# Seven norms of a twelve-stage network: two units multiply the unnormalised input, 1/rms joins their eviction

## The chip, the cores and the metric

The kernel runs on one core of a Trainium2 chip. The metric is the device time of one execution in microseconds (us). The median of three runs of the kernel before is 3014.66 us (3008.84 to 3016.24).

## What is computed

A first network of four layers (pool, neighbourhood attention, conv, pool) works on 512 latent tokens `x` and 256 context tokens `ctx` with 1024 features; a second network of two layers (attention, Fourier mix and gated MLP side by side, then an MLP) works on the result and on another context. What matters here is what stands between the layers:

```python
def _rmsnorm(x, g):
    return x * lax.rsqrt(jnp.mean(x * x, axis=-1, keepdims=True) + EPS) * g

# first network, each of 4 layers
shift, scale, gate = _modulation(c, ada_w[i], ada_b[i])
hx = _rmsnorm(x, norm_g[i]) * (1.0 + scale[:, None]) + shift[:, None]
x = x + gate[:, None] * mixer(hx)          # mixer begins with hx @ w_in
...
return _rmsnorm(x, final_g)

# second network, each of 2 layers
px = modulate(rms_norm(x, g1), sh1, sc1) @ w_in
x = x + gt1 * mix_x
x = x + gt2 * squared_relu_mlp(modulate(rms_norm(x, g2), sh2, sc2), w1, w2)
```

So there are nine norms: one before each of the four mixers, the final one of the first network, and two in each layer of the second. Each is followed by products of the normalised, scaled and shifted `h` with weight matrices.

## The kernel before

Everything is kept transposed: features on the 128 partitions, tokens along the free axis. `x` is eight feature tiles of 512 tokens (`x_lat`) and eight of 256 (`x_ctx`); a stage works on T = TT = 768 tokens or T = TX = 512. Products are made in three passes of a high and a low part: `h_hi`, `h_lo` (names `Hh`, `Hl`) and `w_hi`, `w_lo` (`Wh`, `Wl`), 8 tiles of `h` against 8 tiles of a weight unit of 128x1024. One such product is a *unit*: 128 output features, 8 tiles x 3 passes.

`plan()` writes one list of steps. Each engine runs through that whole list in its order and does its part of every step, so that an engine never takes a later step before an earlier one. The steps that matter:

- `unit` (and `upart`, half of one): PE multiplies into one of two halves of the PSUM tensor `turns` (`PS`); a unit waits (`free_turn`) until the unit two turns back has been evicted. What evicts it depends on `ev`: ScalarE (ACT) for u, v, cg, sk, sq, sf; VectorE (DVE) or both for the rest. After a unit ACT rounds the weight of two units later (`round_unit(w + 2)`, L997) and DVE makes its low part (`split_unit`, L1199, output `w_lo`). There are two buffers for raw weights and two for `w_hi` and `w_lo`.
- `xupd`: the last units of a stage, whose eviction adds gate x product to `x` (DVE, L1202, output `x_lat`, `x_ctx`); ACT squares the new `x` (L1140), DVE adds the squares up in `tmp4` (L1199, output `tmp`).
- `ada` chunks ride on units: DVE multiplies 512 KB of modulation weights with the condition rows (L1213), once or, for sectors with a context row, twice.
- a norm, made by `norm()`: `gain` (DVE, small), `nstat` (PE sums over partitions, L837; ACT square root, L1048; DVE reciprocal and broadcast copy, L1342), `back` (PE transposes, L845, so that `scores` holds 1/rms for each token), then eight `ntile` steps: DVE multiplies x by gain and 1/rms (L1202, output `tmp`), ACT adds the shift and rounds (L1053, output `h_hi`), DVE makes `h_lo` (L1202). `norm()` puts `keep_warm` matmuls (L748) in front of `nstat`.
- the first two units behind a norm are *joined*: PE goes tile by tile through both, the second two tiles behind the first, as the `h` tiles arrive. Before a joined pair stand 8 `keep_warm` calls.
- `pool`: DVE makes windowed means of one u unit; ACT may evict the next u only when DVE is through with it.
- the first network's final norm (`final` steps) multiplies `x` itself, tile by tile, and sums the squares anew for the norm behind it.

In the attention of the first network, each head's bias (128 x 1792) is loaded once by the SyncE queue (SP), into one of two buffers. SP also goes through the list in order: weights (`w + 3` behind unit `w`), ada chunks, biases.

In the code of the mlp units, the eviction is this chain, which the steps of the prediction use:

```python
# ACT
chain(act.activation(T1[:, 0:t], ps[:, 0:t], ACT.Relu))
give(act.activation(Mh[:, m, 0:t], T1[:, 0:t], ACT.Square))
# DVE
chain(tt(T2[:, 0:t], T1[:, 0:t], T1[:, 0:t], ALU.mult))
done(rest(Ml[:, m, 0:t], T2[:, 0:t], Mh[:, m, 0:t]))
```

## Time and profile before

| | |
|---|---|
| median of three runs | 3014.66 us |
| the profiled execution | 3013.29 us, span 3011.5 us |
| PE matmul busy | 2808.6 us, 93% (with the keep-warm matmuls) |
| DVE busy | 1704.4 us, 57% |
| ACT busy | 936.8 us, 31% |
| DMA | 290 MB, mean 96 GB/s |

Times in a timeline are from the start of the span. A row is: start, duration, engine, line, operation, output <- inputs, shapes, how many, and in brackets how long the engine was idle before it and who ended the wait. PEclk is the granted TensorE clock, 1.00 for 2.4 GHz and 0.50 for 1.2 GHz. "turns" in a row is the PSUM tensor of the units, "scores" the other one.

### The profile page before, as it was taken

To read this page: it belongs to the slowest core of one execution; us is meant where nothing else is said; L and a number is where in the kernel's file an instruction comes from. 1 tells how busy PE (TensorE), PEld (TensorE's weight loads), DVE (VectorE), ACT (ScalarE), POOL (GpSimd) and SP (SyncE) were. 2 spreads that over 40 slices of the span, in tenths; PEclk is the share of its full clock that TensorE was granted. 3 is DMA by queue.
4 is the path that set the end of the run, shared out by engine and by line. 5 is a ranking of instruction groups with operands and counts; after the bars stand their busy time and mean duration, and the time that the engine had idled before them with its cause. 6 is when DMAs were issued, how large, how long until landed. Compare 5 with 4: busy or idle time off the path is not lost. (4 is left out here: it accounts for less than half of the span.)

```text
span 3011.5 us, 36579 instructions
## 1 busy us (share of the span) xinstructions
PE 2808.6 (93%) x14298; PEld 2325.1 (77%) x14298; DVE 1704.4 (57%) x2637; ACT 936.8 (31%) x1440; POOL 155.9 (5%) x84
## 2 busy tenths in 40 slices
PE   7998999999999987998988999999999899999999
PEld 6787777787877865776766778888888667878887
DVE  5786656666567878775545465443333546554343
ACT  2222344444232221332334332122122335332222
POOL 0000000000000000000035200000000006200000
PEclk8999999999999998998988999999999999999999
DMA  5242323333245543432300024322212120122333
GB/s 218 84 141 91 127 90 121 121 116 118 67 152 180 190 126 119 141 96 77 126 1 1 29 79 146 125 85 63 64 57 63 54 77 1 43 77 91 98 92 104
DMA packets 81626, 290.02 MB, mean 96 GB/s; under 512 B 9520, under 2 KB 12592, under 8 KB 80944
## 3 DMA queue, kind: packets, MB, share of 16 engines
q1 hardware_dynamic: 81456, 287.69, 29.1%
q8 instruction: 114, 1.87, 0.3%
q14 instruction: 56, 0.46, 0.0%
HBM read 285.56 MB, written 2.10 MB: 96 GB/s over the span
## 5 line engine op out<-in xcount | busy, mean ns | idle before, releaser
L756 PE MATMUL turns<-h_hi,w_hi 128*128 128x512 f32 (+1 forms) x2480 | 803.3, 373 | 70.8 <-DVE w_lo L1199 54.1
L756 PE MATMUL turns<-h_hi,w_lo 128*128 128x512 f32 (+1 forms) x2480 | 782.6, 365 | 0.0
L756 PE MATMUL turns<-h_lo,w_hi 128*128 128x512 f32 (+1 forms) x2480 | 780.0, 364 | 0.0
L756 PEld LDWEIGHTS turns<-h_hi,w_hi 128*128 128x128 f32 x2480 | 425.9, 193 | 178.1 <-DVE w_lo L1199 66.0
L756 PEld LDWEIGHTS turns<-h_hi,w_lo 128*128 128x128 f32 x2480 | 421.5, 192 | 75.0
L756 PEld LDWEIGHTS turns<-h_lo,w_hi 128*128 128x128 f32 x2480 | 422.0, 192 | 73.4 <-issue 1.1
L1199 DVE TENSOR_TENSOR w_lo<-w_raw,w_hi 128x1024 fp32r<-128x1024 f32 x300 | 366.8, 1223 | 141.3 <-ACT w_hi L997 141.0
L997 ACT ACTIVATE w_hi<-w_raw 128x1024 fp32r<-128x1024 f32 x300 | 315.4, 1052 | 384.5 <-PE turns L756 363.3
L711 POOL TENSOR_SCALAR tmp<-tmp,softmax_stats 128x768 f32<-128x768 f32 (+1 forms) x80 | 155.7, 1948 | 2432.6 <-DVE softmax_stats L1429 2432.3
L1202 DVE SCALAR_TENSOR_TENSOR x_lat<-turns,modulation,x_lat 128x512 f32<-128x512 f32 x112 | 84.1, 751 | 335.8 <-PE turns L756 335.8
L756 PE MATMUL turns<-m_hi,w_lo 128*128 128x512 f32 (+1 forms) x768 | 233.4, 358 | 0.0
L756 PE MATMUL turns<-m_hi,w_hi 128*128 128x512 f32 (+1 forms) x768 | 232.8, 357 | 0.0
L756 PE MATMUL turns<-m_lo,w_hi 128*128 128x512 f32 (+1 forms) x768 | 231.5, 356 | 0.0
L1213 DVE CUSTOM_DVE_ANT_0 ada_raw<-ada_raw,cond_rows,ada_bias 128x1024 f32<-128x1024 f32 x176 | 225.3, 1280 | 2.1 <-DMA ada_raw<-in_adapack 1.3
L1199 DVE TENSOR_TENSOR tmp<-tmp 128x768 f32<-128x768 f32 (+4 forms) x88 | 76.5, 870 | 253.9 <-ACT m_hi L1169 253.1
L748 PE MATMUL scores<-dft,ones 128*128 128x256 f32 x500 | 135.9, 421 | 15.7 <-DMA pool_edges<-in_edge 15.7
L756 PEld LDWEIGHTS turns<-m_hi,w_hi 128*128 128x128 f32 x768 | 126.7, 188 | 23.5
L756 PEld LDWEIGHTS turns<-m_lo,w_hi 128*128 128x128 f32 x768 | 126.4, 187 | 23.4
L756 PEld LDWEIGHTS turns<-m_hi,w_lo 128*128 128x128 f32 x768 | 127.4, 188 | 21.4
L1168 ACT ACTIVATE tmp<-turns 128x768 f32<-128x768 f32 (+1 forms) x64 | 45.2, 706 | 291.8 <-PE turns L756 290.0
L1140 ACT ACTIVATE tmp<-x_lat 128x512 f32<-128x512 f32 x56 | 35.4, 632 | 288.8 <-DVE x_ctx L1202 157.4
L748 PEld LDWEIGHTS scores<-dft,ones 128*128 128x128 f32 x500 | 101.6, 212 | 29.7 <-DMA pool_edges<-in_edge 15.7
(212 smaller groups left out, 3408.3 us busy)
## 6 DMA issues: line engine op xcount, KB each, us to landing
w_raw<-in_wpack SPq DMA_DIRECT2D x300, 512.0 KB, 3.5
ada_raw<-in_adapack SPq DMA_DIRECT2D x176, 512.0 KB, 4.4
bias<-in_bias SPq DMA_DIRECT2D x16, 896.0 KB, 4.5
ada_first_a<-in_adapack SPq DMA_DIRECT2D x12, 512.0 KB, 8.6
x_lat<-in_xT SPq DMA_DIRECT2D x1, 2048.0 KB, 9.0
x_ctx<-in_ctxT SPq DMA_DIRECT2D x2, 1024.0 KB, 8.9
ada_first_b<-in_adapack SPq DMA_DIRECT2D x4, 512.0 KB, 15.9
cond_rows<-in_crow SPq DMA_DIRECT2D x4, 512.0 KB, 10.5
```

Source lines behind the costliest of these rows:

```text
L711: pool.tensor_scalar(ex, ex, ST[:, x.qt % 2, 6:7], None, ALU.mult).then_inc(ex_scaled, 1)
L748: pe.matmul(dst, ONES[:], CS[:], start=True, stop=True)
L756: ins = pe.matmul(dst[:, lo:lo + sz], w, x[:, lo:lo + sz], start=first and n == 0, stop=last and n == 2)
L997: act.activation(Wh[:, w % 2, :], RAW[:, w % 2, :], ACT.Copy).then_inc(w_rounded, 1)
L1140: ins = act.activation(T1[:, lo:lo + sz], xseg(lo, m), ACT.Square)
L1168: chain(act.activation(T1[:, 0:t], ps[:, 0:t], ACT.Relu))
L1199: return dve.tensor_tensor(dst, x, y, op)
L1202: return dve.scalar_tensor_tensor(out=dst, in0=x, scalar=c, in1=y, op0=op0, op1=op1)
L1213: ins = dve.tensor_tensor_reduce(dump, ADR[:, n % 2, :], CROW[:, c, :], 0.5, ADAB[:, sect, k:k + 1], ALU.mult, ALU.add, MOD[:, sect, c, k: ...
```

## The change

All norms but the first are made anew, and some things around them:

- Instead of waiting for 1/rms, the first two units behind a norm multiply *raw* tiles: x times gain, rounded by ACT into `h_hi`, with `h_lo` made by DVE (step `raw`, eight of them). If the units before read `h` (src "H"), four or six raw tiles stand in front of the last `xupd` in the list and wait for `h_free`; otherwise one follows each `xupd`.
- The shift rides along as two more columns of `h` (for T = TX, the product is cut into pieces of 256 and 258 columns).
- The sums for 1/rms (`stat_sums`) and the transposes (`stat_back`) are put among the tiles of the raw pair. The eviction of the raw pair (`rawz`) multiplies by 1/rms into `ZT[0]`, `ZT[1]`; `rawb` adds the shift.
- The eight `ntile` steps then write the normalised tiles over the raw ones, each when the raw pair has read its tile, and the third and fourth units are joined instead.
- `w_hi` and `w_lo` get a third buffer: rounding and split go to `w + 3`, loads to `w + 4`. For the room, the attention's bias is loaded in 64 pieces of 128 x 640 into three buffers.
- The final norm of the first network is merged with the norm behind it: a second sum of squares is kept in the updates, and `final` steps multiply `x` later, beside the next units.
- In the attention stages k and v (sk and v) are the raw pair, q and g (sq and sf) the next one; other units shift accordingly. The keep-warm matmuls of these norms and pairs are gone.

```diff
+    def updates(src, T, sect, nxT, after=(), late=False, nxt=None):
+        def raw_tile(k):
+            s = add("raw", T=nxt[2], k=k, g=nxt[0], sect=nxt[1], src=src)
+            s.need = [gain, ups[k]] if k < len(ups) else [gain]
...
+        ahead = 4 if nxt is not None and nxt[2] == TT and T == TT else 6
+        for m in range(KT):
+            if nxt is not None and src == "H" and m == KT - 1:
+                gain = make_gain()
+                for k in range(ahead):
+                    raw_tile(k)
+            u = full(src, "xupd", T, m, after=after if m == 0 else (), sect=sect, nxT=nxT, late=late and m == 0)
...
+            if nxt is not None and src != "H":
+                if m == 0:
+                    gain = make_gain()
+                raw_tile(m)
...
+        for k in range(len(raws), KT - 1 if t == TX or final else KT - 2):
+            raw_tile(k)
+        nst = add("nstat", T=t, g=g, sect=sectn)
...
+        for k in range(len(raws), KT):
+            raw_tile(k)
+        back = add("back", T=t)
...
+        for k in range(KT):
+            tiles.append(add("ntile", T=t, k=k, g=g, sect=sectn))
+            if len(zs) < 2 and k >= (t == TT):
+                zs.append(add("rawz", T=t, half=len(zs)))
...
+        shifted = add("rawb", T=t)
+    def raw_pair(n, u, v):
+        raws, nst, back, tiles, zs, _ = n
+        for j, x in enumerate((u, v)):
+            x.after, x.raw, x.reader, zs[j].of = list(raws), j, zs[j], x
+        u.stats = (nst, back)
...
+        join(u, v)
-            hid = [full("H", "mlp", T, m, after=tiles if c == 0 and m < 2 else ()) for m in range(KT)]
+            hid = [full("H", "mlp", T, m, after=n[3] if c == 0 and m < 4 else ()) for m in range(KT)]
             if c == 0:
-                join(hid[0], hid[1])
+                raw_pair(n, hid[0], hid[1])
+                join(hid[2], hid[3])
-        Wh, Wl = sb("w_hi", [P, 2, D], F32R), sb("w_lo", [P, 2, D], F32R)
+        Wh, Wl = sb("w_hi", [P, 3, D], F32R), sb("w_lo", [P, 3, D], F32R)
...
 # PE
-                if v:
+                if s.warm:
                     keep_warm(8)
                 for x in (s, v) if v else (s,):
                     if x.part != 1:
                         pe.wait_ge(w_split, x.w + 1)
                         free_turn(x)
...
+                    if s.stats is not None and j == 3:
+                        stat_sums(s.stats[0])
+                    if s.stats is not None and j == (6 if s.stats[0].final else 5):
+                        stat_back(s.stats[1])
...
 # ACT
+                elif s.kind == "raw":
+                    act.wait_ge(dve_done, max(x.d1 for x in s.need))
+                    if s.src == "H" and s.k < KT - 1:
+                        act.wait_ge(h_free, (KT - 1) * freeing.index(s.of) + s.k + 1)
+                    for c, (lo, sz) in enumerate(segs(t)):
+                        ins = act.activation(Hh[:, s.k, lo:lo + sz], xseg(lo, s.k), ACT.Copy, scale=GA[:, c, s.k:s.k + 1])
+                    give(ins)
...
 # DVE
+                elif s.kind == "raw":
+                    take()
+                    for c, (lo, sz) in enumerate(segs(t)):
+                        ins = stt(Hl[:, s.k, lo:lo + sz], xseg(lo, s.k), GA[:, c, s.k:s.k + 1],
+                                  Hh[:, s.k, lo:lo + sz].bitcast(F32), ALU.mult, ALU.subtract)
+                    done(ins)
+                elif s.kind == "rawz":
+                    z = ZT[s.half]
+                    dve.tensor_copy(BC[:, s.half, :], ps[:, TT:TT + 2])
+                    if s.half == 0:
+                        chain(dve.tensor_copy(T3[:, 0:t], SP_[:, 0, 0:t]))
+                    if t == TT:
+                        done(tt(z[:, 0:TT], ps[:, 0:TT], T3[:, 0:TT], ALU.mult))
...
+                elif s.kind == "rawb":
+                    for j in range(2):
+                        for c, (lo, sz) in enumerate(segs(t)):
+                            ins = dve.tensor_scalar(ZT[j][:, lo:lo + sz], ZT[j][:, lo:lo + sz], BC[:, j, c:c + 1], None, ALU.add)
+                    done(ins)
...
+                if s.kind == "rawz":
+                    split_unit(s.of.w + 3)
+                if s.kind == "unit" and s.raw is None and turn_of_w[s.w] == s.turn:
+                    split_unit(s.w + 3)
```

## Rows read from the trace of the kernel before

**Rows 1.** The page's first part: busy time of each engine.
```profile
PE 2808.6 (93%) x14298; PEld 2325.1 (77%) x14298; DVE 1704.4 (57%) x2637; ACT 936.8 (31%) x1440; POOL 155.9 (5%) x84
```

**Rows 2.** The waits of PE: who, us in total, times, longest.
```profile
PE turns L756 <- DVE w_lo L1199: 55.0, 32, 7.4
```

**Rows 3.** Stretch 1098 to 1104: PE, PEld, DVE, ACT, POOL busy, then PEclk.
```profile
1098.00:1104.00 6.00, 6.00 (x20) 5.17 (x21) 2.09 (x5) 0.98 (x2) 0.00 (x0) 0.50 0.22 80
```

**Rows 4.** Timeline of the norm before the first MLP, T = 768.
```profile
1768.41 3.62 PE L748 MATMUL scores<-dft,ones 128*128 128x256 f32 x16
1768.71 0.75 DVE L1202 SCALAR_TENSOR_TENSOR x_lat<-turns,modulation,x_lat 128x512 f32<-128x512 f32 x1 [2.71 <-PE turns L756]
...
1770.94 1.03 DVE L1199 TENSOR_TENSOR tmp<-tmp,tmp 128x512 f32<-128x512 f32 x2 [1.08 <-ACT tmp L1140]
1771.89 1.23 DVE L1199 TENSOR_TENSOR w_lo<-w_raw,w_hi 128x1024 fp32r<-128x1024 f32 x1
...
1775.56 0.56 DVE L1342 COPY tmp<-rms 128x768 f32<-128x768 f32 x1
1776.18 1.16 PE L845 MATMUL scores<-ident,tmp 128*128 128x128 f32 x6 [0.39 <-DVE tmp L1342]
...
1777.48 0.75 DVE L1202 SCALAR_TENSOR_TENSOR tmp<-x_lat,gain_cols,scores 128x512 f32<-128x512 f32 x1 [1.36 <-PE scores L845]
...
1779.89 1.15 DVE L1202 SCALAR_TENSOR_TENSOR h_lo<-tmp,modulation,h_hi 128x512 fp32r<-128x512 f32 x2 [0.22 <-ACT h_hi L1053]
...
1796.36 1.15 DVE L1202 SCALAR_TENSOR_TENSOR h_lo<-tmp,modulation,h_hi 128x512 fp32r<-128x512 f32 x2 [1.29 <-ACT h_hi L1053]
```

**Rows 5.** Timeline behind it: evictions of the MLP units; L1168 begins each.
```profile
1799.00 0.81 ACT L1168 ACTIVATE tmp<-turns 128x768 f32<-128x768 f32 x1 [2.77 <-PE turns L756]
...
1802.81 0.81 ACT L1168 ACTIVATE tmp<-turns 128x768 f32<-128x768 f32 x1 [1.17 <-DVE m_lo L1199]
...
1812.84 0.81 ACT L1168 ACTIVATE tmp<-turns 128x768 f32<-128x768 f32 x1 [7.39 <-PE turns L756]
...
1821.32 0.81 ACT L1168 ACTIVATE tmp<-turns 128x768 f32<-128x768 f32 x1 [5.84 <-PE turns L756]
```

**Rows 6.** Timeline, the same stretch of the second MLP, T = 512.
```profile
2638.53 0.75 DVE L1202 SCALAR_TENSOR_TENSOR x_lat<-turns,modulation,x_lat 128x512 f32<-128x512 f32 x1 [1.73 <-PE turns L756]
...
2657.93 0.75 DVE L1202 SCALAR_TENSOR_TENSOR h_lo<-tmp,modulation,h_hi 128x512 fp32r<-128x512 f32 x1 [0.89 <-ACT h_hi L1053]
```

**Rows 7.** Timeline of ACT behind it: the second and the fourth unit's evictions.
```profile
2662.67 0.60 ACT L1168 ACTIVATE tmp<-turns 128x512 f32<-128x512 f32 x1 [0.64 <-DVE m_lo L1199]
...
2676.75 0.60 ACT L1168 ACTIVATE tmp<-turns 128x512 f32<-128x512 f32 x1 [3.23 <-PE turns L756]
```

**Rows 8.** Timeline: conv's seventh and last update on DVE, pool layer's third u on ACT.
```profile
1086.89 0.75 DVE L1202 SCALAR_TENSOR_TENSOR x_lat<-turns,modulation,x_lat 128x512 f32<-128x512 f32 x1
...
1092.91 0.75 DVE L1202 SCALAR_TENSOR_TENSOR x_lat<-turns,modulation,x_lat 128x512 f32<-128x512 f32 x1
...
1136.04 0.60 ACT L1124 ACTIVATE u_padded<-turns 128x512 f32<-128x512 f32 x1 [6.80 <-DVE d_lo L1199]
```

**Rows 9.** Timeline: the pool layer's last update, and the final norm's last sum.
```profile
1308.76 0.75 DVE L1202 SCALAR_TENSOR_TENSOR x_lat<-turns,modulation,x_lat 128x512 f32<-128x512 f32 x1
...
1326.02 0.69 DVE L1199 TENSOR_TENSOR tmp<-tmp,tmp 128x512 f32<-128x512 f32 x1 [0.80 <-ACT tmp L1058]
```

**Rows 10.** Timeline, second network: ends of the eighth unit, each layer (second sf).
```profile
1447.44 0.81 ACT L1160 ACTIVATE fourier_in<-turns 128x768 f32<-128x768 f32 x1 [6.56 <-PE turns L756]
...
2424.12 0.60 ACT L1160 ACTIVATE fourier_in<-turns 128x512 f32<-128x512 f32 x1 [3.89 <-PE turns L756]
```

**Rows 11.** Timeline: DVE at attention's last update before, PE's first transposes behind it.
```profile
326.75 0.75 DVE L1202 SCALAR_TENSOR_TENSOR x_lat<-turns,modulation,x_lat 128x512 f32<-128x512 f32 x1 [2.87 <-PE turns L756]
...
381.61 1.08 PE L899 MATMUL scores<-ident,tmp 128*128 128x128 f32 x4 [2.42 <-DVE v_lo L1199]
```

**Rows 12.** Timeline: one ada chunk on DVE, before the first MLP.
```profile
1764.72 1.28 DVE L1213 CUSTOM_DVE_ANT_0 ada_raw<-ada_raw,cond_rows,ada_bias 128x1024 f32<-128x1024 f32 x1
```

More of the change, by code:

```diff
@@ L77, in __init__ @@
         self.swap = False
+        self.raw, self.stats, self.warm, self.frees, self.need, self.final, self.tiles, self.own = None, None, False, False, [], False, None, False
 ACT_ONLY, DVE_ONLY = {"u", "v", "cg", "sk", "sq", "sf"}, {"cv", "cb"}
@@ L86, in ends_in @@
     if s.kind in ("upart", "scores", "trans", "pvmm", "back", "cond_rows"):
+        return None
+    if s.kind == "unit" and s.ev == "v" and s.raw is not None and s.layer is not None:
         return None
@@ L461, in plan @@
             s.turn = turn
-        elif s.of is not None:
+        elif s.of is not None and s.kind not in ("raw", "rawz", "ntile"):
+            s.turn = s.of.turn
+    for s in steps:
+        if s.kind == "rawz":
             s.turn = s.of.turn
@@ L1017, in _ @@
                 prev = s
[L1018 removed]
+                if s is None or s.kind in ("cond_rows", "upart", "adared", "pool", "spgate", "adape", "scores", "trans", "pvmm", "back", "gnorm", "gain", "adafirst", "rawz", "rawb", "final"):
+                    continue
+                if s.kind == "unit" and s.ev == "v" and s.raw is not None and s.layer is not None:
                     continue
```

386 lines of the change are left out of this document (232 added, 154 removed).

## The prediction

> **What bounds the kernel now.** I read the page first: PE's matmuls are busy for 93% of the span and DVE for 57% [rows 1], so nearly everything costs what it costs PE, except where PE waits. Then PE's waits: the largest in sum is on the low part of a weight, 55 us in 32 waits [rows 2]. Then timelines around the eight norms in question. The one before the first MLP [rows 4] shows the pattern. The last update's matmuls end at 1768.4 (the keep-warm matmuls begin). DVE finishes x and the sum of its squares at 1771.97, PE's transposes of 1/rms begin at 1776.18, and the first tile of h is complete at 1781.0. The last is at 1797.5, so one tile takes (1797.5 - 1781.0)/7 = 2.35 us: an ACT operation and a DVE operation (1.15 us) that wait for each other. The pair that reads them needs 2 x 8 tiles of PE; a whole unit takes 1821.32 - 1812.84 = 8.48 us [rows 5], 1.05 us a tile, so 16.8 us. From 1768.4 to the pair's end, about 1802 (its second eviction begins at 1802.8 [rows 5]), that is 33.6 us for 16.8 us of products. At 512 tokens everything is about two thirds. So the norms do hold idle PE time (some 120 us in sum), but inside them DVE and ACT set the pace, not PE. That decides the rest.
>
> **Norm before the first MLP, step by step (T = 768).** DVE is free 2.71 us before the update starts at 1768.71, so at 1766.0 [rows 4]. New in front of that update: gain and shift columns (six operations on 8 to 16 columns; the nearest row is the copy of 768 columns at 0.56, so below 3.4 and above 0; as they are tiny I take 0.8), ACT's first raw tile (1.1 us, from 0.81 for 768 columns in one operation [rows 5] and two operations here), four raw tiles on DVE at 1.15. They end at 1772.6, so the update, and with it the sum, comes 3.9 us later: at 1775.9. The raw pair can't begin sooner: PE waits for the turn of its second unit, which is that last update. The stretch from 1768.4 to 1775.9 has no keep-warm matmuls any more.
> PE then: four raw tiles 4.2, sums 1.5, four tiles 4.2, transposes 1.1 [rows 4], plus a clock charge of 2.5 (below): 1/rms stands in PSUM at 1789.4. It stood there at 1777.3. The sums' way through ACT and DVE (1776.12 - 1771.97 = 4.15, less 1.35 for split and gain = 2.8) lies beside the second four tiles. From PSUM to the first normalised tile 3.7, as before (1777.3 to 1781.0): 1793.1. Second tile 1795.5. Then `rawz` 1.7 (copy of 1/rms, 0.6 by the copy row of 0.56, and a multiply of 0.96), and because a weight split (1.23) now follows it, the next tile comes 1.2 + 1.15 + 1.15 = 3.5 later; the second `rawz` costs 1.0 and 3.5 again: 1805.2. Four more tiles 9.4: 1814.6. `rawb` (four operations) 1.7: 1816.3. The PE side of the second pair, 16.8 us from 1802, ends at about 1819 to 1820 and is not late.
> What is late next are the evictions, because every engine takes the list in order: the raw pair's outputs may be processed only behind `rawb`. First unit 3.8 (1802.81 - 1799.00 [rows 5]), two ada chunks 2.5 [rows 12], DVE half of the second 1.9, third unit 3.6: 1828.1. PE's fifth unit waits for that turn. It started at 1821.2 (fourth unit's end). Lost: 6.9, and a clock charge of 2.5 since PE sat idle again for 8 us. Term: +9.4.
>
> **The other norms, by the same steps.** Second MLP (T = 512, six raw tiles in front of the update): DVE free at 2638.53 - 1.73 = 2636.8 [rows 6]; 0.8 + 0.6 + 6 x 0.75 gives 2642.7, update 4.2 later, sum at 2644.9; PE 2.8 + 2.5 + 1.0 + 2.8 + 0.7 gives 2654.7; the raw unit's end 3.5 later, 2658.2, now leads: `rawz` 1.2 and 2.7, second 0.8 and 2.7: 2665.6; five tiles at 1.55: 2673.4 (before 2658.7 [rows 6]); `rawb` 1.1; three evictions of 2.8 (2662.67 begins the second [rows 7]): 2682.9 against 2676.5 [rows 7]. Term +6.4 + 2.5 = +8.9.
> Conv: its norm has no raw tiles in front of the update; the eight raw tiles ride in the updates and fit (0.8 lag); then raw pair, tiles, cv's four operations and two chunks before cb frees its turn: 3.5 later, + 2.5 clock. Term +6.0.
> Second pool layer: here DVE is already the bound in the updates before: they start 1092.91 - 1086.89 = 6.02 us apart [rows 8] where PE needs 5.6. Seven raw tiles add 0.75 each, gain, memset and shift 1.7: the sum is 7.0 later. Then 29.5 to the end of `rawb`; u's eviction, chunks and window means follow on DVE. Saved: two rounds and splits (4.6) and 1.2 behind the last u. The third u's eviction, at 1136.04 [rows 8], comes 10 later. Term +8.8.
> Final norm and the one behind: the second square and sum add 1.3 to seven updates (9.2), six raw tiles and gain 9.0: the update of 1308.76 [rows 9] comes at 1327.0, its sum at 1330.5. The final norm's own stretch is gone, which ended at 1326.7 [rows 9]. So this start is 3.8 later, and 46 us behind it four units are done instead of two. Up to the eighth unit (1447.3 before [rows 10]) three unit-and-head steps of 15.5 and one head remain, with `final` (1.5 a step) on DVE in their way: 1449.6. Term +2.3.
> Second network's second layer: no raw tiles in front, evictions on ACT alone; the raw pair covers v, and sk's head, which ran uncovered, lies beside a half unit. Eighth unit at 2419 against 2424 [rows 10]. Term -5.0.
> Neighbourhood attention: free at 326.75 - 2.87 = 323.9 [rows 11], update 3.9 later, `rawb` 40.3 behind the sum: 374.2. Then k, v, q, g are evicted in one go, with five chunks and splits between, and the first softmax has no unit beside it: transposes at 389.9 against 381.6 [rows 11]. Term +8.3.
> Third weight buffer: the long wait of 7.4 [rows 2] shrinks by 2.3 only, since the turn's eviction is late there too; two pool layers save 1.2 each; no other of the 55 us goes, as most lie in the u stretches, where ACT's eviction, round, DVE's split and window means are a closed loop whatever the number of buffers. With small ones, -5. The 64 bias loads have two steps of lead: 0, and up to 1 us on each of 28 ada chunks if a 512 KB load comes late behind them; that stays in the range.
> Sum: 9.4 + 8.9 + 6.0 + 8.8 + 2.3 - 5.0 + 8.3 - 5 = +33.7. Against the profiled execution's own 3013.3 (1.4 below the median) that is 3047.
>
> **The clock charge.** Behind PE's wait that ended at 1097.5 the granted clock is 0.50, 1.2 of 2.4 GHz [rows 3]; the row covers 6 us, in which 3 us of products are lost. The kernel before has keep-warm matmuls against that, which go. I take 2.5 for each restart behind a wait like that one or longer, in seven raw pairs and three restarts behind evictions, 25 us in all; bounds 0 and 3.4 each, 34 in sum.
> The Trainium skill ("TensorE: Matmul & The Clock Gate", What's actually happening) says that for modelling the ramp penalty is under 1% of a typical span. By it alone the charge would be dropped and the sum would be +9, 3022; the row of 0.50 speaks against that for a kernel that adds seven such waits.
>
> **Rivals.** (a) Faster: the raw pair fills PE's idle time and ACT and DVE keep up. That needs the evictions of the raw pair to end before PE's fourth unit; then each norm keeps what its idle time gives, 33.6 less 16.8 less 7.5 that remain in front, some 9 us at 768 and 5 at 512 tokens, and the final norm's 16: near 65, so 2950 to 2990. For it: half of each norm is idle PE. Against it: the tile pace of 2.35 us starts 12 us later and has 5.7 us of `rawz` and splits in it. "Perfetto Trace Analysis" (Optimization Strategies) of the Trainium skill has this rule, to keep the matmul engine utilised and to relieve the engine that blocks; the first half speaks for the change, the second against it, since DVE gets more work. (b) No difference: restarts cost nothing, or the list hides the evictions better than I count: +9 to -9, 3004 to 3022. (c) Worse than forecast, and slower than before: the SP queue, which now waits for each softmax step, hands ada chunks out late; from about 3 us of delay DVE waits in each of 28 units: +30 on top, 3077.
>
> **Chances and numbers.** Forecast (slower, 3030 to 3066) 0.68; (a) 0.16; (b) 0.12; (c) 0.04. A measurement of this kernel tells 0.3%, 9 us, from no change. Faster 0.16, same 0.12, slower 0.72. Range 2992 to 3066: it leaves out (c) and most of (a); the forecast's own is 3030 to 3066.
>
> **What would show it.** In the profile after: first tile of h (L1202) some 12 us later behind each sum; the update in front of the raw pair starting 4 us behind PE's end; PE waiting for evictions (an `m_lo`, a `conv` operation) before the fifth unit; DVE's busy time up by some 90 us; 0.50 clocks behind each norm. If PE's fifth unit starts without a wait, (a) is true. If updates of the conv layer stay 6.0 us apart, the pool term is wrong.

## The result, and the profile after

The changed kernel takes 3080.27 us (median of four, 3077.68 to 3092.32), before 3015.45 beside it: ratio 1.0217 [1.0193, 1.0241]. Timed once more later, it was 1.0207 [1.0184, 1.0229]. So it is 62 to 65 us slower, where 34 were forecast; the direction was right, the size was not, and 3080 lies above the forecast's range (2992 to 3066). The profiled execution took 3082.5 us, its span is 3080.7.

The changed kernel's page, answering to [rows 1], and then the mean granted clock of before and of the changed kernel:

```profile
PE 2775.9 (90%) x14134; PEld 2307.7 (75%) x14134; DVE 1786.1 (58%) x2814; ACT 984.5 (32%) x1526; POOL 155.9 (5%) x84
```
```profile
core 0: 3011.5 us, clock 0.960
```
```profile
core 0: 3080.7 us, clock 0.945
```

PE is busy 33 us less (the keep-warm matmuls are gone), DVE 82 us more (forecast about 90). PE's waits by line and releaser (us in total, times, longest), answering to [rows 2]:

```profile
PE turns L817 <- DVE tmp L1317: 66.4, 16, 17.7
PE turns L817 <- ACT u_padded L1239: 36.1, 10, 12.6
PE turns L817 <- DVE raw_out L1317: 28.5, 7, 6.5
PE scores L940 <- DVE tmp L1527: 26.8, 14, 4.9
```

The 55.0 us for the low part of a weight are gone. In their place stand waits that the forecast named: for the sum of squares in front of the raw pair (seven of the 16 waits for `tmp` L1317, 56.4 us of the 66.4), and for the raw pair's first output (`raw_out`), seven times, once a norm.

PE's busy time from the first product of `h` to the end; the columns are the stretch, its length, PE busy (matmuls), clock, DMA share and GB/s. Before, then the changed kernel:

```profile
69.96:3011.50 2941.54, 2758.26 (x14024) 0.96 0.29 93
```
```profile
78.92:3080.70 3001.78, 2714.99 (x13860) 0.95 0.29 93
```

So PE is idle 287 us there in place of 183: the change adds 104 us of waits and takes away 43 us of busy time, keep-warm matmuls above all.

The norm before the first MLP in the changed kernel, answering to [rows 4] and [rows 5]; a bracket at a PE row is its wait:

```profile
1826.39 0.75 DVE L1320 SCALAR_TENSOR_TENSOR x_lat<-turns,modulation,x_lat 128x512 f32<-128x512 f32 x1
...
1829.90 0.98 PE L817 MATMUL turns<-h_hi,w_hi 128*128 128x512 f32 x2 [7.67 <-DVE tmp L1317]
...
1843.27 0.75 DVE L1320 SCALAR_TENSOR_TENSOR tmp<-x_lat,gain_cols,scores 128x512 f32<-128x512 f32 x1 [1.15 <-PE scores L841]
...
1845.74 1.15 DVE L1320 SCALAR_TENSOR_TENSOR h_lo<-tmp,modulation,h_hi 128x512 fp32r<-128x512 f32 x2 [0.28 <-ACT h_hi L1171]
...
1867.26 1.15 DVE L1320 SCALAR_TENSOR_TENSOR h_lo<-tmp,modulation,h_hi 128x512 fp32r<-128x512 f32 x2 [1.29 <-ACT h_hi L1171]
1868.51 1.42 DVE L1469 TENSOR_SCALAR raw_out<-raw_out,raw_shift 128x512 f32<-128x512 f32 x4
...
1882.36 0.98 PE L817 MATMUL turns<-h_hi,w_hi 128*128 128x512 f32 x2 [7.74 <-DVE m_lo L1317]
```

The update stands behind four raw tiles, 4.1 us after PE's last product of it (1822.2). The sum stands at 1829.65 (the row of x is followed by its square and the sum, 3.3 us). From there the first normalised tile is complete 17.2 us later and the last 38.7 us, to the tenth what the forecast has (1775.9 to 1793.1 and 1814.6); that some ten steps add up to the tenth is luck, that they stand in this order is not. PE waits 7.67 us (forecast 7.5) for the raw pair, reads the last normalised tile by 1874.6, and then waits 7.74 us for the eviction that frees the fifth unit's turn (forecast 8 to 9: from 1819 or 1820 to 1828.1).

Here the steps of the forecast can be read off one by one. The other terms come from marks: the first update of `x` on DVE in each stage. The table gives them in us. The shift is taken from the first product of `h`, which is 9.0 us later in the changed kernel's profile (78.92 against 69.96; see the section on the hardware). "Of this step" is the shift less that of the row above, so a row holds the norm in front of its stage and the rest of the stretch between the two marks.

| first update of | before | after | shift | of this step | forecast |
|---|---|---|---|---|---|
| first pool layer | 267.4 | 276.1 | -0.3 | -0.3 | third buffer |
| neighbourhood attention | 804.0 | 823.2 | 10.2 | 10.5 | 8.3 |
| conv | 1050.7 | 1077.7 | 18.0 | 7.8 | 6.0 |
| second pool layer | 1266.5 | 1307.0 | 31.5 | 13.5 | 8.8 |
| second network, first attention | 1710.5 | 1763.2 | 43.7 | 12.2 | 2.3 |
| first MLP, first block | 1863.7 | 1926.8 | 54.2 | 10.5 | 9.4 |
| first MLP, fourth block | 2269.4 | 2329.5 | 51.1 | -3.1 | third buffer |
| second attention | 2600.5 | 2655.5 | 46.1 | -5.0 | -5.0 |
| second MLP, first block | 2704.1 | 2769.5 | 56.4 | 10.3 | 8.9 |
| second MLP, fourth block | 2969.1 | 3038.1 | 60.1 | 3.7 | third buffer |

The seven norms cost 59.8 us against 38.7 forecast; the rest, which the forecast put at -5 for the third buffer, is +0.3. In a second profile of the changed kernel each step is within 0.2 us of these, but for the first, 3.2 us larger. So a mark is good to about 3 us, and so is a sum of them. The marks give 60 us and the times 62 to 65; where the rest lies is open, since the profiles tell nothing of the other executions.

### The profile page after: what moved, and what is told of

The parts are those of the page before. It is cut to its first block and busy times, and to the rows that moved or that the text cites. A ratio compares the mean times of both kernels' runs of the same rounds, so it can differ in the third digit from the quotient of the medians.

```text
span 3080.7 us, 36741 instructions
## 1 busy us (share of the span) xinstructions
PE 2775.9 (90%) x14134; PEld 2307.7 (75%) x14134; DVE 1786.1 (58%) x2814; ACT 984.5 (32%) x1526; POOL 155.9 (5%) x84
## 5 line engine op out<-in xcount | busy, mean ns | idle before, releaser
L817 PE MATMUL turns<-h_hi,w_hi 128*128 128x512 f32 (+1 forms) x2528 | 817.3, 375 | 163.2 <-DVE tmp L1317 60.2
L817 PE MATMUL turns<-h_lo,w_hi 128*128 128x512 f32 (+1 forms) x2528 | 801.0, 369 | 0.0
L817 PE MATMUL turns<-h_hi,w_lo 128*128 128x512 f32 (+1 forms) x2528 | 797.6, 367 | 0.0
L817 PEld LDWEIGHTS turns<-h_hi,w_hi 128*128 128x128 f32 x2528 | 442.1, 198 | 261.8 <-issue 180.6
L817 PEld LDWEIGHTS turns<-h_lo,w_hi 128*128 128x128 f32 x2528 | 440.2, 197 | 78.1 <-issue 1.5
L817 PEld LDWEIGHTS turns<-h_hi,w_lo 128*128 128x128 f32 x2528 | 439.3, 196 | 78.5
L1317 DVE TENSOR_TENSOR w_lo<-w_raw,w_hi 128x1024 fp32r<-128x1024 f32 x300 | 366.7, 1223 | 108.2 <-ACT w_hi L1092 108.1
L1317 DVE TENSOR_TENSOR tmp<-tmp 128x768 f32<-128x768 f32 (+4 forms) x88 | 76.5, 870 | 245.2 <-ACT m_hi L1287 244.3
L1331 DVE CUSTOM_DVE_ANT_0 ada_acc<-ada_raw,cond_rows,ada_bias 128x1024 f32<-128x1024 f32 x88 | 112.6, 1280 | 2.2 <-DMA ada_raw<-in_adapack 1.3
L1317 DVE TENSOR_TENSOR pt_lo<-turns,pt_hi 128x768 fp32r<-128x768 f32 (+1 forms) x80 | 67.9, 849 | 61.1 <-ACT pt_hi L1201 59.9
## 6 DMA issues: line engine op xcount, KB each, us to landing
cond_rows<-in_crow SPq DMA_DIRECT2D x4, 512.0 KB, 10.3
```

The lines of the kernel that those rows point to most:

```text
L817: ins = pe.matmul(dst[:, at:at + sz], w, x[:, lo:lo + sz], start=first and n == 0, stop=last and n == 2)
L1317: return dve.tensor_tensor(dst, x, y, op)
L1331: ins = dve.tensor_tensor_reduce(dump, ADR[:, n % 2, :], CROW[:, c, :], 0.5, ADAB[:, sect, k:k + 1], ALU.mult, ALU.add, MOD[:, sect, c, k: ...
```

## Experiments

All ratios are to the kernel before, timed beside each. "By the marks" is the shift of the last mark from before, as in the table (60.1 for the changed kernel, 63.2 in its second profile); it comes from one execution, the ratio from four or more. Where the two differ, both are given.

### The parts that are not norms

All eight norms as before on the changed kernel, so that the third weight buffer, the loads four units ahead and the bias pieces are left:

```diff
+        if nxt is not None and nxt[0] in OLD:      # OLD = (1, 2, 3, 4, 5, 6, 7)
+            for m in range(KT):
+                full(src, "xupd", T, m, ...)
+            return old_norm(nxt[2], nxt[0], nxt[1])
```

> All eight norms as before; only the third buffer of w_hi and w_lo, the loads four units ahead and the 64 bias pieces of the change are kept. Theory A (the prediction's term): 5 us faster than before, 3010, with the 7.4 us wait for w_lo in the conv layer gone. Theory B (from the two traces: the attention steps keep their pitch, the MLP blocks at 768 tokens gain 1.0 each, those at 512 lose 1.2 each, the conv stage loses 2): between 0 and 3 us slower, 3015 to 3018. The start of the program, whose instructions are the same in all kernels, took 9 us longer in the changed kernel's profile: if the buffers or the bias do that, it is here too, and the time is 3024.

Measured 0.9994 [0.9976, 1.0013], by the marks -2.5 us: no difference that the times show, and neither theory is excluded by them alone. The 7.4 us wait of the conv layer is still 4.9, as the forecast had it (2.3 less). But PE's idle time from the first product of `h` on is 180 us (183 before): where PE waited for `w_lo` in the pool layers, it now waits about as long for ACT's eviction of the u before (`u_padded`). So the savings that the forecast had there didn't come. (In this kernel and the next the weights of the attention stages lie in another order than the units, so these layers multiply by each other's columns; their operations are those of the right order.)

With this run as the base in place of before, the seven norms cost 11.2, 9.1, 12.3, 11.9, 10.3, -3.3 and 11.0 us in the order of the table, 62.5 in sum.

The same with `OLD = (1, 2, 3, 4, 6, 7)`, one norm new:

> As the run with the buffers alone, but the norm ahead of the second network's second layer is made the changed kernel's way (raw pair sk and v, then sq and sf). The traces of before and after give a term of -5.1 us for that stretch and +5.6 us for the stage behind it, of which 4.2 were forecast. Theory A (the terms are local): 5 us faster than the run with the buffers alone. Theory B (the gain is given back in the half units and attention steps behind it): within 2 us of it.

1.0015 [0.9996, 1.0034], by the marks -5.2, that is 2.7 us less than the run above: by the times no difference can be told. The marks put it in the norm's own stretch (-5.2 there against -1.7), and the stretches behind it gain or lose nothing more. Even the one norm that gained is no gain that a measurement shows.

### The place of the tiles

```diff
-        Hh, Hl = sb("h_hi", [P, KT, TT + 2], F32R), sb("h_lo", [P, KT, TT + 2], F32R)
+        Hh, Hl = sb("h_hi", [P, KT, TT], F32R), sb("h_lo", [P, KT, TT], F32R)
```

> The run with the buffers alone (all eight norms as before, third weight buffer, 64 bias pieces), but with h tiles 768 words apart, as before, in place of 770: the two shift columns that only the changed norms need are gone. In the trace of the run with 770, a product of 512 columns of h starts 225 to 240 ns after the one ahead of it, in a pattern that repeats every eight tiles; in the trace of before it is 227 ns always. Theory A (the place of the tiles in memory sets the pace of the products): 2480 products of 512 columns get 4.5 ns faster and some 700 tiles of 768 tokens 4 ns, 14 us in all: 3002 where before has 3016. Theory B (the third weight buffer makes the pattern): as the run with 770 words, 2 us faster than before.

0.9959 [0.9942, 0.9975], by the marks -17.5: theory A, and this kernel is faster than before and than the changed kernel. Two stretches of eight units in the second MLP (192 products of 512 columns each, nothing else on PE), first of `h`, then of `m`, with the columns as above. Before, then the run with 770 words, then 768:

```profile
2743.02:2786.55 43.53, 43.53 (x193) 1.00 0.28 86
2786.55:2831.34 44.79, 44.79 (x193) 1.00 0.33 105
```
```profile
2742.57:2787.15 44.58, 44.58 (x194) 1.00 0.29 85
2787.15:2832.12 44.97, 44.97 (x193) 1.00 0.34 104
```
```profile
2730.98:2774.51 43.53, 43.53 (x193) 1.00 0.30 86
2774.51:2819.49 44.98, 44.98 (x193) 1.00 0.34 105
```

At the same clock and with PE never idle, eight units of `h` take 43.53 us with tiles 768 words apart and 44.58 with 770: 227 and 232 ns a product. That is the price of the room for the shift columns at 512 tokens, and the forecast had nothing for it. At 768 tokens, where pieces of 512 and 256 columns take turns, it isn't paid everywhere: a block of the first MLP takes 134.4 us with 768 words and 134.2 with 770.

What makes the 12 us against before is not the waits either. From the first product of `h` on, with 770 and with 768 words:

```profile
75.52:3014.70 2939.18, 2758.71 (x14024) 0.97 0.30 95
```
```profile
75.84:3000.00 2924.16, 2738.45 (x14024) 0.97 0.30 96
```

PE is idle 180 and 186 us (183 before), and busy 2759 and 2738 (2758 before). So the gain lies in the pace of the products, part of it in less half clock, and not in fewer waits for a buffer. Such a run also moves all other tensors: the block of the first MLP, in which PE is never idle, went from 135.3 us to 134.4 with them. How much of the 12 us is owed to the third buffer and how much to the places, no run took apart.

With 800 words in the changed kernel:

> The changed kernel with h tiles 800 words apart in place of 770, nothing else. Theory A (the place of the tiles in memory sets the pace): 11 to 14 us faster than the changed kernel. Theory B (pace set by the three weight buffers): no change. Either way the waits of the norms stay as they are.

1.0196 [1.0163, 1.0229], by the marks 63.1: nothing, and eight units of `h` keep their mean of 232 ns a product. This excludes neither the place of the tiles nor the buffers as the cause: 800 words, like 770, put the eight tiles at eight different places modulo 1024 bytes, 768 words at one. With 768 words and the shift columns left out:

> The changed kernel with h tiles 768 words apart and without the two shift columns in the products: the raw pairs' outputs lack the shift (a column of the product stands in for it, so that every other operation is the same). With 800 words in place of 770 nothing had changed. Theory A (only with 768 words, the same place modulo 1024 bytes for each tile, do products of h start every 227 ns; the kernel with norms as before gained 15 us by it): 12 to 15 us faster than the changed kernel. Theory B (in the changed kernel the waits of the norms hide it, since its products of h stand partly in them): 5 us or less.

1.0155 [1.0135, 1.0175], by the marks 53.0: 16 to 19 us less than the changed kernel by the times, 7 by the marks. Eight units of `h` in the second MLP, in the changed kernel and here:

```profile
2808.54:2853.11 44.57, 44.57 (x193) 1.00 0.28 85
```
```profile
2801.82:2845.38 43.56, 43.56 (x193) 1.00 0.27 86
```

The pace comes back in the changed kernel too, with its three buffers, so the place of the tiles makes it. Whether it is worth 7 or 17 us these runs don't settle.

In the fast kernel (768 words, norms as before), all later tensors moved by 864 bytes:

> The kernel with the norms as before, third weight buffer and h tiles 768 words apart (0.9959 of before), with all tensors of the later stages moved by 864 bytes, so that the m tiles lie at the same place modulo 1024 bytes as the h tiles, whose products at 512 columns start every 227 ns; those of m start every 234 ns now. Theory A (place modulo 1024 bytes sets the pace): the products of m at 512 columns go to 227 ns, 5 us, and the time to 0.994 of before. Theory B (h and m differ for another reason, say what wrote them): pace and time stay.

0.9948 [0.9928, 0.9968], by the marks -14.7: as fast as without it. But the pace did as said; `m`, then `h`:

```profile
2696.67:2740.19 43.52, 43.52 (x193) 1.00 0.34 107
2740.19:2783.71 43.52, 43.52 (x193) 1.00 0.28 87
```

The products of `m` at 512 tokens went from 44.98 us to 43.52 by their place alone. At 768 tokens the same move made them slower (a block of the first MLP takes 135.7 us, 1.3 more), and both about cancel.

### The clock

> The changed kernel with keep-warm matmuls put in front of the raw pair, the second pair and the fifth unit of each norm, about as many as fill 80% of PE's wait there. Theory A (the clock charge of 2.5 us a restart, 25 in the sum): 15 to 25 us faster than the changed kernel, 3055 to 3065. Theory B (ACT and DVE set the pace of these stretches, so that PE's half clock behind a wait is mostly hidden in waits that follow): 5 us or less, 3075 to 3080.

1.0291 [1.0267, 1.0314], by the marks 87.7: 22 to 25 us slower than the changed kernel by the times, so neither theory is tested. One keep-warm call is two matmuls; they outlasted the waits and held PE up (around the first MLP's norm PE isn't idle at all). With 40% as many, and then once more beside the changed kernel:

```diff
+                if s.keep:
+                    keep_warm(s.keep)              # 12, 6, 12 at the first MLP norm
```

> As the run with keep-warm matmuls, which was 23 us slower than the changed kernel since each call is two matmuls and the calls outlasted the waits; here 40% as many (12, 6 and 12 at the first MLP norm), so that they end inside the waits. Theory A (the clock charge, 2.5 us a restart): 15 to 25 us faster than the changed kernel. Theory B (ACT and DVE set the pace of these stretches): 5 us or less.

> The changed kernel itself once more, beside the three kernels of this call, so that they are compared on one chip. Its profile tells how far two executions of the same instructions differ: the start (until the first product with h) took 70.0 to 79.3 us in the profiles so far, and the time that PE's products lose at half clock behind it 98 us in before and 115 in the changed kernel. If those are chance, both move here; if the change makes them, they stay at 79 and 115.

> The changed kernel with keep-warm matmuls that end inside the waits, as before, timed beside the changed kernel. Its profile had 16.5 us less of products at half clock than the changed kernel's, and the same span behind the first product; its times were 0.44% lower, with an interval as wide. Theory A (the clock charge is real, about 16 us of it): 10 to 16 us faster than the changed kernel. Theory B (ACT and DVE set the pace, so that nothing is gained): within 4 us of it.

Changed kernel again: 1.0207 [1.0184, 1.0229], by the marks 63.2. With keep-warm: 1.0173 [1.0142, 1.0204] and 1.0175 [1.0155, 1.0195], so 10 to 13 us less each time, though the intervals still overlap. By the marks it is 60.5 and 55.8, 0 to 7 us less: 4.4 less in the conv step and 2.8 in the first MLP's, both times, but 4.2 more in the second attention's. The first MLP's norm in the second of these, with PE's waits in front of the raw pair, the second pair and the fifth unit:

```profile
1823.57 0.59 PE L827 MATMUL turns<-h_hi,w_hi 128*128 128x512 f32 x2 [2.49 <-DVE tmp L1329]
1847.12 0.59 PE L827 MATMUL turns<-h_hi,w_hi 128*128 128x512 f32 x2 [1.74 <-DVE raw_out L1329]
1873.50 0.98 PE L827 MATMUL turns<-h_hi,w_hi 128*128 128x512 f32 x2 [4.07 <-DVE m_lo L1329]
```

Two of three restarts now go at full clock (0.59 us for two products, not 0.98), and from the raw pair to the fifth unit it is 49.9 us, where it was 52.5. What is lost to half clock can be added up in two ways, from the first product of `h` on. PE's busy time, times the share of the clock that wasn't granted, is 98 us in before, 121 and 123 in the two profiles of the changed kernel, 102 in both with keep-warm. What the pace of gapless products loses against the usual one of their kind is 98, 115 and 116, and 99, a sum that hangs on what is taken as usual. So the change loses 17 to 25 us of products to half clock, and at most some 10 to 13 of them are time. The charge is real; 25 was about twice too much.

The Trainium skill ("TensorE: Matmul & The Clock Gate", What's actually happening) puts the ramp penalty under 1% of a typical span. For what the change adds this holds: 10 to 13 us are 0.3 to 0.4% of 3080. For all of it it doesn't: 98 us are 3.3% of the span of before. By the page alone the sum was 3022, further from what came than with the charge.

The changed kernel's second profile also has a first product of `h` at 79.0 us, as the first had. By the expectation that would make the late start the change's own. But kernels with the changed norms have theirs at 69.2 to 70.1 us in three other profiles, and one with the norms as before at 79.1: the start isn't the change's. The half clock is.

### DVE's list in front of the sum

```diff
-        ahead = 4 if nxt is not None and nxt[2] == TT and T == TT else 6
+        ahead = 2
```

> The changed kernel with two raw tiles in front of the last update in place of four (768 tokens) or six (512). In the trace of after, DVE is free 2.5 us ahead of the update in front of the first MLP and four raw tiles then hold the update up 4.1 us. Theory A (the raw tiles in front of the update are the delay): 2.5 to 3 us less in each of the four norms concerned, 3068 to 3071. Theory B (raw tiles behind the update then hold up the raw pair as much): no change, 3080.

1.0158 [1.0135, 1.0181], by the marks 48.1: 15 to 18 us less by the times, 12 by the marks: 0.1, 6.9, 3.1 and 3.7 in the steps of the four norms with such tiles, and 2.2 more in the first pool layer, which the edit doesn't touch. (In the neighbourhood attention the wait in front of the raw pair is 2.5 us shorter, but the step isn't.) PE's wait in front of the first MLP's raw pair is now

```profile
1812.84 0.98 PE L817 MATMUL turns<-h_hi,w_hi 128*128 128x512 f32 x2 [5.18 <-DVE tmp L1317]
```

against 7.67. So theory A: the raw tiles put in front of the last update were a delay, and those behind it weren't late.

### DVE's list behind the raw pair

```diff
+        elif skip[0]:                              # skip[0] = 4 behind each norm
+            skip[0] -= 1
+            owed[0] += 1
+            chunks = 0
```

> The changed kernel, but the first four units behind each of the seven norms take no modulation chunk; later units take two until the debt is paid. In the trace of after, DVE has two chunks (2.7 us) between the shift step and the eviction for which the fifth unit of the MLP waits, and ten chunk operations (12.8 us) ahead of the first head's 1/rms in the second network's first layer. Theory A (DVE's list behind the raw pair is the path): 15 to 25 us faster than the changed kernel. Theory B (the debt costs as much later, or ACT is the path): within 5 us.

Both theories fall: 1.0248 [1.0227, 1.0269], 12 us slower than the changed kernel. The fifth unit of the first MLP still waits 7.03 us (7.74), so the chunks there were hardly on the path. The loss is mostly in the second network's heads. By the marks (74.0) the first attention takes 10.6 us more than in the changed kernel; the neighbourhood attention takes 4.9 more and the conv step 3.7 less, and why is open. PE's head sums there, for sk and sq0 to sq3, in the changed kernel and in this one:

```profile
1420.23 1.39 PE L948 MATMUL scores<-head_ones,sk_square 128*128 128x2 f32 x12
1439.97 1.39 PE L948 MATMUL scores<-head_ones,tmp 128*128 128x2 f32 x12
1454.41 1.40 PE L948 MATMUL scores<-head_ones,tmp 128*128 128x2 f32 x12
1471.96 1.39 PE L948 MATMUL scores<-head_ones,tmp 128*128 128x2 f32 x12
1490.75 1.40 PE L948 MATMUL scores<-head_ones,tmp 128*128 128x2 f32 x12
```
```profile
1423.82 1.39 PE L953 MATMUL scores<-head_ones,sk_square 128*128 128x2 f32 x12
1436.74 1.39 PE L953 MATMUL scores<-head_ones,tmp 128*128 128x2 f32 x12
1457.24 1.40 PE L953 MATMUL scores<-head_ones,tmp 128*128 128x2 f32 x12
1477.68 1.39 PE L953 MATMUL scores<-head_ones,tmp 128*128 128x2 f32 x12
1498.12 1.39 PE L953 MATMUL scores<-head_ones,tmp 128*128 128x2 f32 x12
```

The first step is shorter (12.9 us from 19.7, no chunks ahead of it), but the three behind it went from 14.4, 17.6 and 18.8 to 20.4 or 20.5: two chunks, both twice, now stand ahead of each head's 1/rms on DVE. In sum that is 3.8 us more; the other 7 lie in front of these rows and behind them, and were not taken apart. The debt was moved, in part, to where DVE is the path.

### The final norm

The final norm and the one behind it as before, `OLD = (4,)`:

> The changed kernel with the first network's final norm and the norm behind it made as before, one after the other, and the second network's first layer in its old order of units. From the start of the pool updates to the first update behind the attention, the changed kernel is 12 us slower than the one with all norms as before; the forecast had 2.3. Theory A (raw tiles in front of the last pool update, six heads' steps with modulation chunks and final steps in front of them on DVE): 10 to 13 us faster than the changed kernel. Theory B (the stretch behind catches up): under 5 us.

1.0179 [1.0148, 1.0209], 9 to 11 us less than the changed kernel: theory A by the times. By the marks it is 14 less at the first attention's update and at the end of the first MLP, but only 3.6 at the end: in the second attention of this execution 8 us more than in before's are lost at half clock, in the changed kernel's 1.5 us less. That looks like chance of the execution and not like the edit, since the kernel with three edits below, which has this one too, has -3.6 us in that step; no second profile was taken.

In the next kernel the final norm is merged again, and its eight `final` steps stand further back:

```diff
-            if both and len(finals) < KT:
-                finals += [add("final", k=len(finals) + j, T=TX) for j in range(2)]
+            if both and e == "su":
+                finals += [add("final", k=len(finals) + j, T=TX) for j in range(4)]
```

> The changed kernel, but the eight final steps of the merged norm (each pair 1.6 us on DVE) stand behind the units su0 and su1, where no head follows, and not in front of four heads' 1/rms. The step from one unit to the next was 17.6 to 18.8 us there against 15.5 forecast. Theory A (the final steps are in the heads' way): 5 to 7 us faster than the changed kernel. Theory B (the half units wait for ACT and PE's half clock, not for DVE): under 2 us.

1.0211 [1.0189, 1.0232]: nothing by the times. By the marks it is 71.7, 8 to 12 us slower than the changed kernel, 6.5 of them in the first attention's step. And yet theory B is wrong, which had the final steps in nobody's way. The same head sums, sk to sq3, and the transposes behind them:

```profile
1418.71 1.39 PE L948 MATMUL scores<-head_ones,sk_square 128*128 128x2 f32 x12
1438.30 1.40 PE L948 MATMUL scores<-head_ones,tmp 128*128 128x2 f32 x12
1451.20 1.39 PE L948 MATMUL scores<-head_ones,tmp 128*128 128x2 f32 x12
1466.82 1.39 PE L948 MATMUL scores<-head_ones,tmp 128*128 128x2 f32 x12
1480.73 1.40 PE L948 MATMUL scores<-head_ones,tmp 128*128 128x2 f32 x12
...
1514.14 1.54 PE L957 MATMUL scores<-ident,raw_out 128*128 128x128 f32 x6 [10.76 <-DVE x_lat L1320]
```

From the second one on, the sums are 12.9, 15.6 and 13.9 us apart (the last two 14.8 and 13.8 in before), and from the first to the last it is 8.5 us less than in the changed kernel. So the final steps were in their way. But the final steps now hold the part of `scores` that the next transposes need, and PE waits 10.76 us for that: a gain turned into new waits that are at least as long.

### Sums of edits

The norms of the conv layer and of the second pool layer as before, `OLD = (2, 3)`:

> The changed kernel with the norms in front of the conv layer and of the second pool layer made as before, the other five in the new way. In the traces the two terms are 9 and 12 us (forecast 6.0 and 8.8), the conv updates being 7.2 us apart in place of 6.0. Theory A (the terms are local): 18 to 22 us faster than the changed kernel, 1.0140 of before. Theory B (part of them is lost again behind them): 12 us or less.

1.0134 [1.0114, 1.0153], by the marks 39.2: 22 to 25 us less by the times, 21 to 24 by the marks, with 9.5 less in the conv step and 12.7 in the second pool layer's. Theory A: these terms are local.

Two tiles ahead, keep-warm and the final norm apart, together:

> The three edits that helped alone, together: two raw tiles in front of the last update (-15 us by the ratios), keep-warm matmuls that end inside the waits (-10), the final norm apart (-9). Theory A (they work in different places and add up): 1.0207 - 0.0050 - 0.0032 - 0.0030 = 1.0095 of before, 3048. Theory B (ACT and DVE behind the raw pair are the bound, and what one mend gives the next one loses): 1.013 or more.

1.0126 [1.0109, 1.0144], by the marks 34.9: 24 to 27 us less by the times, where the three alone sum to between 33 and 42. That lies between the two theories: part of it adds up, part doesn't, and the interval leaves open how much. Even so this kernel is 38 us slower than before, and 50 behind the kernel with 768 words, which has no raw pair.

## Why the prediction was right, and where it was wrong

**What bounds the norm.** Right: not PE but the tile pace of DVE and ACT, and the evictions behind it. PE idles 7.67, 4.33 and 7.74 us in the first MLP's norm, in front of the raw pair, the second pair and the fifth unit, where the kernel before kept it warm or busy. So rival (a), which had PE's fifth unit start without a wait, is excluded, and (b) by the times.

**First and second MLP, attention.** 9.4, 8.9 and 8.3 forecast, 10.5, 10.3 and 10.5 measured. The mechanism stands (the update 4.1 us behind PE, forecast about 4; the fifth unit's wait in the MLPs). In the MLPs the run with two tiles ahead changes what the steps said it would. Only the sizes are 1 to 2 us short. One of the signs was put wrongly: the first tile of `h` is 12 us later on the clock in the forecast, but behind the sum it is 17.2 us in place of 9.0, so 8 later.

**Second attention.** -5.0, as forecast, but in part by luck: 1.8 of it is there with the buffers alone, and by the run with this norm alone the rest isn't worth a difference that the times show.

**Conv and second pool layer.** 6.0 and 8.8 forecast, 7.8 and 13.5 measured; the run without both confirms the sum. The conv updates were taken as 7 x 0.75 later; they are

```profile
1114.33 0.75 DVE L1320 SCALAR_TENSOR_TENSOR x_lat<-turns,modulation,x_lat 128x512 f32<-128x512 f32 x1
...
1121.20 0.75 DVE L1320 SCALAR_TENSOR_TENSOR x_lat<-turns,modulation,x_lat 128x512 f32<-128x512 f32 x1
```

6.87 us apart, 0.85 more than in [rows 8], and PE is now idle 1.0 us in each, so the raw tile is on the path with its whole length and a little more, and the last update is 8.2 us late (forecast 7.0). At the forecast's own mark, ACT's eviction of the third `u`, it was nearly right: 10.9 us late (1173.91 against 1136.04, less 9.0 and 18.0), 10 forecast. But the 1.2 us that it saved behind the last `u` don't come (the eighth is still 10.9 late), and 2.6 us are added behind the `u` units, 1.2 of them with the buffers alone too. What the other 1.4 are no run took apart. In the conv step 9.8 us are lost at half clock, 2.2 before, where one charge of 2.5 had been taken.

**The final norm: the step that failed most.** 2.3 forecast, 12.2 measured. The 9.9 us between them come about in four steps (times of the changed kernel less the 40.5 us by which all is late there: 9.0 and 31.5):

- The raw pair starts at 1327.9, forecast 1330.5: 2.6 us to the good. PE's longest wait, 17.7 us, stands in front of it.
- The fourth unit's eviction by ACT begins at 1378.7, forecast 1376.5. From the raw pair's start it took 50.8 us and not 46: 4.8 too little.
- From there, four more units and the last head took 76.9 us (ACT's eviction of the ninth unit begins at 1504.37, and that unit is 8.3) and not 73.1 (1449.6 less 1376.5): 3.8 too little. The steps that the forecast names (three of 15.5, 1.5 for the final steps in each, one head) don't show how 73.1 came about. On PE the heads' sums are 14.4, 17.6 and 18.8 us apart where final steps stand between them, and 19.7 in front of the first, where ten chunk operations stand. A pair of final steps is 1.6 us on DVE and cost up to 5 (18.8 against 13.9 without it).
- Behind the last head the forecast took nothing; 4.1 us more are lost there, in the su and sgv units and the Fourier mix. Why is open.

So the sum went wrong in what stands behind the raw pair: DVE's list was costed by the length of its entries, not by the waits that they make on PE. The runs show that this is the place. With the final norm apart the first attention's step is 14 us shorter. With the final steps late the heads come 8.5 us sooner, and other waits take it back.

**The clock charge.** Mis-sized: 25 us forecast, against 17 to 25 us of lost products and 10 to 13 us of time at most. With the charge at its measured size the forecast would have been 12 to 15 us further off; this error hid a part of the others.

**The third buffer.** Forecast -5, from shorter waits; +0.3 measured. The long wait did shrink as forecast (7.35 to 4.95 us), but the pool layers' savings didn't come, and the products of `h` at 512 tokens got slower: in the conv step of the run with the buffers alone PE is idle 4.4 us less and busy 3.1 more. This is the term that the forecast didn't have at all: it costed the shift columns as small operations on DVE, and not what two more words between the tiles do to the pace of the products that read them. With tiles 768 words apart the same parts give 12 us by the times (17 by the marks), in pace and not in waits.

**SP's queue, the rival at 3077.** The number came close, the mechanism not: the attention's half units and softmax steps keep their pitch (from the second pair on 321.3 us against 320.8 for six pairs), and the run with the bias pieces and no raw norm is no slower than before. All of DVE's waits for a chunk's load are 4.4 us in the changed kernel.

The sum, put right by these: norms 59.8 (21.1 more than forecast: 9.9 the final norm, 4.7 the second pool layer, 6.5 the other five), the rest 0.3 (5.3 more), so 3013.3 + 60.1 = 3073.4, and the start, which was 9.0 us later in the profiled execution, makes its 3082.5.

## What to carry to other kernels

A unit that starts before its scale is known saves PE's wait only if the engines that evict it have room behind it; here DVE and ACT set the pace of the norm already, and every raw tile, every scaled eviction and every final step is one more entry in lists that are worked off in order, in front of something that PE needs. Before a step is moved, look for what stands behind it in its new place: chunks and final steps moved out of one path landed in another, twice. And when a tile grows by two words, look at the pace of all products that read it, in a stretch where PE has no gap; and before a gain is put down to a buffer, see whether PE's idle time fell.

## What the runs showed of the hardware

**The pace of a product hangs on where its operands lie.** At the granted clock 1.00, without gaps, products of 512 columns follow each other every 224 to 242 ns. At 512 tokens, with `h` tiles 3072 bytes apart, it is 226 or 227 each time; with 3080 or 3200 bytes it goes through a pattern from 225 to 240 that repeats after eight tiles, mean 232. Moving `m` by 864 bytes took it from a mean of 234 to 227, and at 768 tokens it took the 512-column pieces from 229 to between 232 and 241. There `h` tiles 3072 bytes apart don't have the even pace either: their 512-column pieces take 233, 236 and 241 ns in the three passes. What modulo 1024 bytes decides (the tile against the weights, or against the one before) no run took apart. The Trainium skill ("TensorE: Matmul & The Clock Gate", Step-by-step: what each phase is for) says that loading the next weights doesn't steal read bandwidth from the running product. No run here tests that by itself; the place of operands in memory costs a single product up to 6%.

**The start isn't the same twice.** The instructions up to the first product of `h` are the same in all kernels, and take 69.2 to 79.3 us. Six keep-warm matmuls at the start, first at the slow and then at the fast pace; before, then the changed kernel:

```profile
15.71 2.93 PE L748 MATMUL scores<-dft,ones 128*128 128x256 f32 x6 [15.71 <-DMA pool_edges<-in_edge]
...
20.30 1.54 PE L748 MATMUL scores<-dft,ones 128*128 128x256 f32 x6
```
```profile
33.02 2.91 PE L809 MATMUL scores<-dft,ones 128*128 128x256 f32 x6
...
37.85 1.54 PE L809 MATMUL scores<-dft,ones 128*128 128x256 f32 x6
```

PE works without a gap from its first matmul to 36 us in both, on the same list. It doubles its pace at 18.8 us in before, some 3 us behind that matmul, and at 36.6 us in the changed kernel, some 21 us behind it. These are the times at which the records of the granted clock begin, with 1.00. A view of a stretch in front of the first record prints 1.00 too, so there the pace of the matmuls tells the level, and not the clock column. In all eighteen profiles the first product of `h` follows this time: a rise at 18.1 to 19.3 us has it at 69.2 to 70.1, one at 24.2 at 72.7, one at 29.7 to 30.8 at 75.5 to 76.1, one at 36.3 to 36.8 at 78.9 to 79.3. What sets the time of the rise no run shows. The Trainium skill (same page, What's actually happening) says that the number of slow products at the start differs between runs of one kernel; these profiles, of kernels with the same start, agree. By these profiles it can make 10 of the 25 us over which the times of before spread in one set (3005.7 to 3031.0), and it is why profiles should be compared from their first product of `h` on.
